# A fourth block of shift columns moved from TensorE to VectorE, and two feature tiles reordered, in the first stage of a two-block model kernel

## What is computed

```python
c_act = jax.nn.silu(c)
mod = c_act @ ada_w[i] + ada_b[i]
sh1, sc1, g1, sh2, sc2, g2 = [t[:, None, :] for t in jnp.split(mod, 6, axis=-1)]
h = _rms(x) * (1.0 + sc1) + sh1
# in _rwkv7_mix, with x = h
xx = _token_shift(x) - x
xs = x[None] + xx[None] * mix[:, None, None, :]
r = xs[0] @ w_in[:, 0:1024]          # then w, k, v, a, g from xs[1] to xs[5]
```

## Time and profile before

| | us |
|---|---|
| median of 3 runs | 2500.04 |
| fastest, slowest of them | 2498.82, 2507.3 |
| the profiled execution | 2501.76 |
| its span in the trace | 2499.7 |
| busy in it: TensorE matmul, VectorE, ScalarE, GpSimd | 2424.1, 1595.6, 1083.8, 541.3 |
| mean granted TensorE clock | 0.992 of 2.4 GHz |

### The profile page before, as it was taken

One profiled execution on the slowest core, in us unless ns is written; L12 is line 12 of the kernel. 1 busy time (PEld: TensorE's weight loads), 2 busy tenths in 40 slices (PEclk: granted clock), 3 DMA queues, 4 the chain that ended last, 5 costly groups with the idle time before them and its releaser, 6 DMA issues.

```text
span 2499.7 us, 37777 instructions
## 1 busy us (share of the span) xinstructions
PE 2424.1 (97%) x15774; PEld 2017.2 (81%) x15774; DVE 1595.6 (64%) x2225; ACT 1083.8 (43%) x1621; POOL 541.3 (22%) x190
## 2 busy tenths in 40 slices
PE   8998989999999999999999999999999999999999
PEld 7746875798989888789999878999877877777776
DVE  6578868787867875488666653666427526666505
ACT  6653544453534435454434432332334335544523
POOL 1321203100000344510000034233133433111132
PEclk9999999999999999999999999999999999999999
DMA  7223353234444342124222322121222222111121
GB/s 289 84 93 71 72 147 148 85 138 166 141 155 165 130 178 76 68 85 169 100 103 102 119 90 101 68 85 68 76 90 100 84 85 101 68 52 68 60 93 59
DMA packets 94409, 264.26 MB, mean 106 GB/s; under 512 B 55200, under 2 KB 55840, under 8 KB 69280
## 3 DMA queue, kind: packets, MB, share of 16 engines
q1 hardware_dynamic: 91936, 253.46, 29.5%
q10 hardware_dynamic: 2304, 8.39, 0.9%
HBM read 256.05 MB, written 5.78 MB: 105 GB/s over the span
## 4 chain that ended last, share of the span: by engine, by line
PE 74%; DVE 14%; ACT 5%; issue 3%; DMA 3%; POOL 1%; SPq 0%; DVEq 0%; ACTq 0%; POOLq 0%
PE bank L356 13%; PE bank L358 13%; PE bank L357 13%; PE bank L2567 5%; PE bank L2569 5%; PE bank L2570 5%; PE bank L289 2%; PE bank L287 2%; PE bank L288 2%; DVE q_rope L4635 1%; PE bank L4099 1%; PE bank L4412 1%; ACT w_high L377 1%; DVE ada_slot L697 1%; POOL ring_low L387 1%
## 5 line engine op out<-in xcount | busy, mean ns | idle before, releaser
L387 POOL TENSOR_TENSOR ring_low<-ring,w_high 128x2048 fp32r<-128x2048 f32 (+1 forms) x102 | 465.2, 4562 | 1716.5 <-ACT w_high L377 1716.5
L377 ACT ACTIVATE w_high<-ring 128x2048 fp32r<-128x2048 f32 (+1 forms) x134 | 247.0, 1849 | 267.1 <-PE bank L358 255.4
L356 PE MATMUL bank<-h_high,w_high 128*128 128x512 f32 (+1 forms) x584 | 234.5, 402 | 0.7 <-DVEq L3940 0.7
L358 PE MATMUL bank<-h_high,ring_low 128*128 128x512 f32 (+1 forms) x584 | 231.9, 397 | 0.0
L357 PE MATMUL bank<-h_low,w_high 128*128 128x512 f32 (+1 forms) x584 | 230.6, 395 | 0.0
L356 PE MATMUL bank<-z_high,w_high 128*128 128x512 f32 x380 | 151.4, 398 | 5.1 <-DVE z_low L4593 1.5
L358 PE MATMUL bank<-z_high,ring_low 128*128 128x512 f32 x380 | 150.5, 396 | 0.0
L357 PE MATMUL bank<-z_low,w_high 128*128 128x512 f32 x380 | 149.9, 395 | 0.0
L358 PE MATMUL bank<-hidden_high,ring_low 128*128 128x512 f32 x352 | 139.5, 396 | 0.0
L356 PE MATMUL bank<-hidden_high,w_high 128*128 128x512 f32 x352 | 139.5, 396 | 0.0
L697 DVE SCALAR_TENSOR_TENSOR ada_slot<-ada_slot,c_row 128x1024 f32<-128x1024 f32 x73 | 108.8, 1502 | 47.5 <-DMA ada_slot<-in_ada_next 20.5
(11 more groups left out here) (559 smaller groups left out, 6523.0 us busy)
## 6 DMA issues: line engine op xcount, KB each, us to landing
ring<-in_stream SPq DMA_DIRECT2D x186, 1024.0 KB, 4.8
ada_slot<-in_ada_next SPq DMA_DIRECT2D x40, 512.0 KB, 4.2
ada_slot<-in_gains SPq DMA_DIRECT2D x17, 512.0 KB, 4.6
ada_slot<-in_first SPq DMA_DIRECT2D x16, 512.0 KB, 4.3
scale_weights<-in_first SPq DMA_DIRECT2D x4, 1024.0 KB, 22.7
inverse<-scratch_inverse SPq DMA_DIRECT2D x32, 128.0 KB, 3.1
x_res<-in_x SPq DMA_DIRECT2D x2, 1024.0 KB, 7.8
w_first<-in_first SPq DMA_DIRECT2D x2, 1024.0 KB, 15.6
```

Source lines behind the costliest of these rows:

```text
L356: pe.matmul(out, w_high[:, k, cols], x_high, start=start, stop=False)
L358: return pe.matmul(out, w_low[:, k, cols], x_high, start=False, stop=stop)
L377: act.activation(self.high_buf[:, b % 2, 0:cols], self.c.ring[:, b % SLOTS, 0:cols], ACT.Copy)\
L387: pool.tensor_tensor(self.c.ring_low[:, b % SLOTS, 0:cols], self.c.ring[:, b % SLOTS, 0:cols], self.high_buf[:, b % 2, 0:cols].bitcast(F32 ...
```

## The change

Three things are changed.

Shift block 3 is no longer a matmul block. The host lays its weights out transposed, as those of the scale already are (`ada_blocks(i, 3, 4)` has tiles 6 and 7 of the conditioning weights). They still land in ring slot 3. VectorE makes the two columns with two `ada_tile` in a new `last_shift`, which stands where `shift_pair(3)` stood, and adds the bias.

On TensorE `shift_block(3)` is gone. Since no matmul now frees slot 3, TensorE waits after tile 5 for the shift columns and then adds two to `gemm_done` by itself.

The last two feature tiles of the first half of r are taken feature by feature: all four outputs for k = 6, then all four for k = 7.

```diff
-    unit, shift_mm, shift = Step(chip, "rw_unit", KD), Step(chip, "rw_shift_mm", 4), Step(chip, "rw_shift", 4)
-    summed, scale, normed = Step(chip, "rw_summed", 8), Step(chip, "rw_scale", 4), Step(chip, "rw_normed", KD)
+    unit, shift_mm, shift = Step(chip, "rw_unit", KD), Step(chip, "rw_shift_mm", 3), Step(chip, "rw_shift", 4)
+    summed, scale, normed = Step(chip, "rw_summed", 10), Step(chip, "rw_scale", 4), Step(chip, "rw_normed", KD)
...
         def shift_block(i):
             chip.wait_block(pe, b_sh + i)
             pe.wait_ge(silu.sem, silu.of(1))
-            if i == 3:
-                pe.wait_ge(shift.sem, shift.of(0))
...
                 if k == 0 and n == 1:
                     shift_block(2)
-            if k == 1:
-                shift_block(3)
-        for n in range(4):
-            for k in range(KD - 2, KD):
-                if n == 0:
-                    ready("r")(k)
+        pe.wait_ge(shift.sem, shift.of(3))
+        pe.sem_inc(chip.gemm_done, 2)
+        for k in range(KD - 2, KD):
+            ready("r")(k)
+            for n in range(4):
                 mm = first(k, n)
-            mm.then_inc(first_done.sem, 1)
+                if k == KD - 1:
+                    mm.then_inc(first_done.sem, 1)
...
+        def last_shift():
+            chip.wait_block(dve, b_sh + 3)
+            for j in range(2):
+                ada_tile(chip, dve, chip.ring[:, (b_sh + 3) % SLOTS, j * D:(j + 1) * D], KD - 2 + j)\
+                    .then_inc(summed.sem, 1)
+            dve.wait_ge(summed.sem, summed.of(9))
+            dve.tensor_tensor(chip.mod[:, KD - 2:KD], chip.mod[:, KD - 2:KD], chip.v("ada_b")[:, KD - 2:KD], ALU.add)\
+               .then_inc(shift.sem, 1)
+
         def shift_pair(i):
+            if i == 3:
+                return last_shift()
...
-    return [weight_blocks(i["ada_w"][0][:, :D], KD, 2 * P), weight_blocks(rwkv_weights(i, "r")[:, 4 * P:], KD, 2 * P),
+    return [weight_blocks(i["ada_w"][0][:, :6 * P], KD, 2 * P), *ada_blocks(i, 3, 4), weight_blocks(rwkv_weights(i, "r")[:, 4 * P:], KD, 2 * P),
```

## The result

The changed kernel took 2508.72 us in the median (2504.0 to 2515.05, 20 runs), the kernel before 2501.05 us (2497.03 to 2507.71, 20 runs) beside it. The ratio is 1.0026, with a 95% interval of 1.0017 to 1.0035. So the change makes the kernel slower by about 6.5 us (the means lie 6.6 us apart, the medians 7.7). That lies inside the 0.3% that I had called no difference, but outside the forecast's range: 2508.72 against 2502.4 (2497.8 to 2507.5). The profiled execution took 2505.66 us, with a span of 2503.8 us.

The account below looks back on a forecast made before the run. It took VectorE and ScalarE, without slack from 42.64 us on, to bound the changed stretch, TensorE the rest. Two sums (2.29 us) and a wait (0.11) gave +2.40 on the median 2500.04: 2502.4 us, range 2497.8 to 2507.5.

Parts of the forecast that it names:

- the sum of the first stage: VectorE's two `ada_tile` (2.29 us) plus the bias addition's wait (0.11) delay the first stage by 2.40 us.
- the restart: TensorE starting the second half of r after ScalarE's first two evictions: moves from 59.94 to 62.34 us.
- ScalarE's row: ScalarE's gapless instructions from 50.32 to 59.80 us, through the evictions: move as a whole, by 2.40 us.
- idle before tile 5: In the first half of r, TensorE stands from 46.3 to 50.7 us, 4.4 us, waiting for tile 5.
- TensorE's 3.88 us: Work saved by removing shift block 3 at 37.70 us: all becomes idle time, none reaches the end.
- the order: Tiles 6 and 7 feature by feature in the first half of r: costs nothing.
- block 7's load: Load into ring slot 3, issued at about 53.5 instead of 41.55 us: lands by 80.2 at worst, cost zero.
- The fall of the clock in the first gap: Lower clock after the idle time before tile 5: 1.5 us, hidden by the wait until 62.34.
- Rival 2: TensorE's relief in the first half of r counts: 2.0 us faster, 2498.0 us; chance 0.04.
- Rival 3: Delay absorbed behind 105 us by a transfer not depending on TensorE: 2500.0 us; chance 0.10.
- the one from the restart to the end: Behind 59.94 us, a shift of TensorE's restart shifts all that follows; no further term was added.
- rival 1: Clock falls at 62.3 to 66 us: 1.5 us, or 3.0, more; 2503.9, up to 2505.4; chance 0.22.

Follow-up runs that it names:

- order_only: Kernel before with only tiles 6 and 7 taken feature by feature, shift block 3 still on TensorE: ratio 0.9992.
- warm_fill: Changed kernel with TensorE's idle time before tile 5 filled by 16 spare products, and 6 more before the second half of r: ratio 1.0024.
- again_after: The changed kernel, unchanged, run a second time against the kernel before: ratio 1.0028.
- sums_left_out: Changed kernel without VectorE's two sums, so the shift columns of tiles 6 and 7 are only twice the bias: ratio 1.0026.
- before_padded: Kernel before with 16 spare products on TensorE ahead of its first wait in the first stage's second half: ratio 1.0022.
- one_sum: Kernel before with one unused sum of 1.15 us added on VectorE ahead of the last pair of shift columns: ratio 1.0009.
- four_sums: Kernel before with four unused sums, 4.6 us, added on VectorE ahead of the last pair of shift columns: ratio 1.0021.
- sums_added: Kernel before with two unused sums added on VectorE ahead of the fourth shift pair, shift block 3 still on TensorE: ratio 1.0022.
- after_padded: Changed kernel with 16 spare products on TensorE ahead of its first wait in the first stage's second half: ratio 1.0021.
- after_evict: Changed kernel with ScalarE's first two evictions of r moved up, behind the third of its eight tiles for k: ratio 1.0019.
- after_warm_evict: Changed kernel with the first two evictions of r moved up and 16 spare products in TensorE's first gap: ratio 1.0001.

## Why the prediction was right, and where it failed

**Right, to a tenth of a microsecond: the sum of the first stage.** Two sums at 2.29 us and a wait of 0.12 (forecast 0.11); `norm` of tile 6 at +2.41 and the restart at +2.38 (2.40); ScalarE's row moved as a whole; 4.14 us idle before tile 5 (4.4) and 1.65 before the restart (3.1, less the fall of the clock in between). TensorE's 3.88 us were worth nothing there, the order nothing (order_only 0.9992), and block 7's load, issued at 52.27 instead of 41.55, was waited for by nobody. The fall of the clock in the first gap cost 1.3 us of matmul time ((54.86 - 52.14) less 6 x 0.235; forecast 1.5) and was hidden by ScalarE; warm_fill took it away without moving the restart. Rival 2 falls with again_after. Rival 3 falls too: the 2.4 us were not absorbed, since every kernel with two sums more on VectorE and the evictions where they were was 2.2 us or more slower at equal loss.

**Wrong: what follows behind the first stage.** The step that failed is the one from the restart to the end. The prediction wrote that a shift of TensorE's restart shifts all that follows, ended its sum at the restart, and so gave the rest of the program a term of zero. The term measured about 4 us. For again_after the account is: +6.4 in all, of which 2.4 is the delay; lost clock +5.2 us at 0.65, so 3.4; and 0.6 left, with an error of 0.7. The split is no finer than that: of the 5.2 us lost, 1.7 is the fall in the first gap, which costs nothing, and the slope is a mean over kernels. For warm_fill it doesn't hold: +5.0 in all, 2.4 of delay, 0.4 of lost clock, and 2.2 left. I had put the clock into rival 1 at 1.5 to 3.0 us and had the kind of cost right for again_after, but tied it to one place, the restart. There the clock was 1.00 in both traces of the changed kernel; at that place it fell in sums_left_out, before_padded and one_sum. Lost clock has to be priced over the whole program, from the mean clock of all executions, and not at the one gap that the change opens.

**The range.** 2508.72 is 1.2 us above its upper end. Of the 6.3 us by which the forecast missed, 1.0 is the kernel before itself, whose median is 2501.05 over 20 runs where three runs had given 2500.04. Another 4.1 is the term above (6.5 less 2.4), and the last 1.2 is that the medians lie 7.7 us apart where the ratio says 6.5. The chance of 0.05 for over 0.3% slower is fair for a ratio of 1.0026 with an end at 1.0035; what was too narrow is the range, since no rival let two things go wrong together.

**Open.** Why a first stage that is late by 2.4 us, or has a fall of the clock in it, is followed by more lost time in the chunk stage is not settled. What the runs show is an association: of the table's eight kernels in whose trace the clock fell before 70 us, six lost 4 to 6 us more over the whole program than the kernel before (one_sum and four_sums 1.6 and 3.1), and the others never more than 2.2. The idle times behind which it falls later (1.5 to 3.7 us, from 152, 231, 408, 419 and 1458 us on in the kernel before) are there in the changed kernel too. The excess is not in proportion to the delay (four_sums), and it doesn't need the block missing on TensorE (sums_added and before_padded have it and cost as much); that the placement of instructions has a part of up to a microsecond is not excluded (after_padded). For warm_fill and sums_added, the longer wait for the round trip at 272 us fits the 1.4 to 2.2 us that lost clock leaves over, but what makes it longer is not shown.

## What to carry to other kernels

Ask of work moved between engines which of the two has slack at that place, as read from the chain; 3.88 us off an engine with 1.2 us of slack gave nothing, and 2.29 us on one without slack cost all of itself. A gap that such a move opens is not free even where it is hidden: it can cost clock, and it takes the cover from the next edit (at the next stage after_evict got 0.4 us where after_warm_evict got 2.6). Where the expected effect is a tenth of a per cent, put the clock's scatter into the range, and compare lost clock beside the times. And look early for a mark behind the change that all kernels share: it says which part of the program to search.

## What had not been expected of the hardware

- Over 387 executions of nearly equal kernels 1 us of lost clock went with 0.65 us of span, and at one place, with the fall there and without it, 1.7 us of lost clock made 1.1 to 1.5. The kernel before loses 20.8 us, so by the slope some 14 us of its 2500 hang on it, an estimate. A fill of 28 spare products in two gaps went with 2.1 us less (+- 1.2).
- The fall behind one and the same gap is not certain. At the restart of the second half of r, with up to 2.9 us idle before it, the clock fell in three kernels and stayed full in the others; of the two with 2.93 us, it fell in sums_left_out and not in sums_added.
- Spare products on an idle TensorE can do harm: 16 of them ahead of the first products made the kernel before 1.0022 times as long, with the clock in its trace at 0.66 from 17 to 22 us, where it had been 1.00. In after_padded the same products did no such harm.
- An idle time of 1.63 us that nothing released, inside a run of equal matmuls, was gone when 16 products were added ahead of it, 265 us earlier. The 32 matmul records of a block, present or absent at 38 us, went with the line at which such a stall stood some 330 us later.
- Beside GpSimd's subtraction of two blocks VectorE nearly stands still. Its two mixes, 0.75 us each otherwise, took 7.98 us, in the kernel before as well (54.57 us); the two timelines of the kernel after:

```profile
56.10 9.70 POOL L387 TENSOR_TENSOR ring_low<-ring,w_high 128x2048 fp32r<-128x2048 f32 x2 [54.32 <-ACT w_high L377]
```

```profile
58.37 7.98 DVE L1200 SCALAR_TENSOR_TENSOR rw_all<-h,vec,rw_all 128x512 f32<-128x512 f32 x2 [3.53 <-ACT rw_all L1062]
```
